# The second block's banded attention: scores as three float32r products of depth 64, two heads on the two row halves of the array

## The reference

```python
q, k, v = ...                      # of h @ w_in: (b,l,16*64), (b,l,4*64), (b,l,4*64)
s = einsum("bnqgrd,bnkgd->bgrnqk", qb, kb) * 64 ** -0.5      # 128 queries x 384 keys
valid = (abs(dist) <= 128) & (key >= 0) & (key < l)
s = where(valid, s - slopes * abs(dist), -inf)               # slope of head h: 2 ** (-8 (h+1) / 16)
m = maximum(max(s), sink)                                    # sink: one logit per head
p = exp(s - m)
probs = p / (sum(p) + exp(sink - m))
o = einsum("bgrnqk,bnkgd->bnqgrd", probs, vb)
```

## Time and profile before

| | us |
|---|---|
| median of 3 executions | 3427.03 |
| lowest, highest | 3340.12, 3492.56 |
| span of the profiled execution | 3498.2 |
| TensorE busy in it | 2989.8 (85%) |
| VectorE busy | 1504.5 (43%) |
| ScalarE busy | 972.0 (28%) |
| mean granted TensorE clock | 0.854 |

### The profile page before, as it was taken

The page is one execution under the profiler, slowest core; times in us unless marked ns, Lnnn a source line. Parts: engine busy times, 40 slices in busy tenths (PEclk is TensorE's granted clock), DMA queues, the critical chain, the costliest instruction groups (busy, mean ns, idle before and its releaser), DMA issues. The chain is left out here.

```text
span 3498.2 us, 37554 instructions
## 1 busy us (share of the span) xinstructions
PE 2989.8 (85%) x13760; PEld 2374.7 (68%) x13760; DVE 1504.5 (43%) x3662; ACT 972.0 (28%) x2200; POOL 196.1 (6%) x203
## 2 busy tenths in 40 slices
PE   3999957999565939899999998896696699999996
PEld 3888846779454728766666885772584588887875
DVE  3111367667888131244444114558413341424244
ACT  2121242446543121232222123450311321212121
POOL 1000020000200010000000000226000000000000
PEclk8999865999797969855555999699798799999998
DMA  2121200000001221000000120001213111111113
GB/s 83 49 73 50 86 1 1 1 1 2 1 1 48 97 74 50 19 7 13 7 13 34 49 73 28 1 1 54 82 49 118 43 48 49 49 49 46 50 47 117
DMA packets 91655, 144.86 MB, mean 41 GB/s; under 512 B 34256, under 2 KB 40528, under 8 KB 91472
## 3 DMA queue, kind: packets, MB, share of 16 engines
q1 hardware_dynamic: 84304, 117.28, 11.0%
q0 software_dynamic: 4864, 16.78, 1.2%
q10 hardware_dynamic: 2304, 8.39, 0.6%
HBM read 117.25 MB, written 25.17 MB: 41 GB/s over the span
## 5 line engine op out<-in xcount | busy, mean ns | idle before, releaser
L368 PE MATMUL banks<-h3T,mlwhi 128*128 128x512 f32 x1024 | 318.4, 392 | 9.4 <-DVE mlwlo L334 6.1
L368 PE MATMUL banks<-mlwhi,fT 128*128 128x512 f32 x1024 | 316.1, 390 | 3.3 <-ACT relu L2140 3.3
L368 PE MATMUL banks<-g1whi,hT 128*128 128x512 f32 (+1 forms) x1024 | 302.0, 378 | 5.7 <-DVE g1wlo L334 5.7
L334 DVE TENSOR_TENSOR mlwlo<-mlraw,mlwhi 128x512 fp32r<-128x512 f32 x128 | 87.7, 691 | 464.4 <-ACT mlwhi L311 464.4
L368 PEld LDWEIGHTS banks<-h3T,mlwhi 128*128 128x128 f32 x1024 | 192.9, 189 | 52.6 <-DVE mlwlo L334 6.5
L311 ACT ACTIVATE mlwhi<-mlraw 128x512 fp32r<-128x512 f32 x128 | 80.8, 632 | 526.9 <-PE banks L368 522.6
L368 PEld LDWEIGHTS banks<-mlwhi,fT 128*128 128x128 f32 x1024 | 191.6, 188 | 45.7 <-ACT relu L2140 6.3
L368 PEld LDWEIGHTS banks<-g1whi,hT 128*128 128x128 f32 x1024 | 189.2, 189 | 41.3 <-DVE g1wlo L334 6.1
L1053 PE MATMUL banks<-k2T,q2T 64*128 64x384 f32 (+1 forms) x256 | 194.1, 870 | 9.7 <-PEq L1495 9.7
L368 PE MATMUL banks<-h3T,mlwlo 128*128 128x512 f32 x512 | 200.1, 391 | 0.0
L368 PE MATMUL banks<-mlwlo,fT 128*128 128x512 f32 x512 | 199.2, 389 | 0.0
(11 more groups left out here) (448 smaller groups left out, 5760.2 us busy)
## 6 DMA issues: line engine op xcount, KB each, us to landing
mlraw<-in_w_up SPq DMA_DIRECT2D x64, 256.0 KB, 2.8
mlraw<-in_w_down SPq DMA_DIRECT2D x64, 256.0 KB, 2.7
g1raw<-in_w_in SPq DMA_DIRECT2D x56, 256.0 KB, 2.6
g3raw<-in_w_in SPq DMA_DIRECT2D x40, 256.0 KB, 2.6
g4raw<-in_w_out SPq DMA_DIRECT2D x32, 256.0 KB, 2.6
xt<-in_x SPq DMA_DIRECT2D x8, 512.0 KB, 6.6
z_scratch<-zst POOLq DMA_DIRECT2D x16, 256.0 KB, 2.6
cw<-in_cmp_w SPq DMA_DIRECT2D x2, 2048.0 KB, 9.2
```

The lines of the kernel that those rows point to most:

```text
L334: nc.vector.tensor_tensor(wlo[n % RING][:, w_slice(n)], raw[n % RAW][:, w_slice(n)], f32(whi[n % RING][:, w_slice(n)]), ALU.subtract).then ...
L368: last = nc.tensor.matmul(out, l, r, start=(k == 0 and i == 0), stop=(k == job.nk - 1 and i == 2))
```

## The change

In g2, q and k are kept as float32r pairs: `q2T` and `k2T` become two tensors each, high part written by ScalarE, low part by VectorE (product minus high part), for every accumulator. A query row half holds head j and the other half head j+8, so that the k job needs each key head once: 256 columns, four accumulators, where there were 512 and eight. q is scaled by 0.125 / slope of its head, with a table `qscale` that 16 small memsets write in a block of its own ahead of g2. The weights of the q jobs come in two transfers a step with 256-byte pieces.

The ALiBi table is one [128, 384] tile without slopes; the custom operation multiplies by the negated slope instead and takes a minimum.

The attention has its own function, `window2_stage`. Scores are issued for two heads together: three float32r products of depth 64 for each, alternating between the row halves, in two PSUM banks. Values are 64 columns wide. The sink's exp, the sum, the reciprocal and the scaling are done for four heads at once. VectorE's copy of the transposes of u-2 stands behind the bias operations of u+3 and u+4.

```diff
 def window2_tables(nc, sem, mem, C, kb, tmp_kb):
-            for h in range(ATT_HEADS):
-                nc.vector.tensor_scalar(tab[:, h, :], base[:], 2.0 ** (-8.0 * (h + 1) / ATT_HEADS), None,
-                                        ALU.mult).then_inc(dve_s, 1)
+            nc.vector.tensor_copy(tab[:], base[:]).then_inc(dve_s, 1)
+def window2_stage(nc, sem, mem, ident, q_hi, q_lo, k_hi, k_lo, v2, tab, nsink, x_kb, pt_kb, st_kb, yt, y_free, psum,
+                  store):
+    X, AHEAD, LAG = 6, 4, 2
...
+            def scores(u):
...
+                if u >= 4:
+                    pe.wait_ge(m_ready, u - 2)
+                for n, (q, k) in enumerate(((q_hi, k_hi), (q_hi, k_lo), (q_lo, k_hi))):
+                    for b in range(2):
+                        rows = slice(64 * b, 64 * b + 64)
+                        last = nc.tensor.matmul(psum[(u + b) % 4][:, 0:width(u)], q[rows, j, tok],
+                                                k[rows, j // 4, keys_at], start=(n == 0), stop=(n == 2))
+                        if n == 2:
+                            last.then_inc(s_ready, 1)
+            def transposes(u):
+                pe.wait_ge(e_ready, u + 1)
+                if u >= 2:
+                    pe.wait_ge(dev if u % 2 else aev, u // 2)
...
+            def values(u):
+                t, h = divmod(u, ATT_HEADS)
+                k0, k1 = keys(u)
+                pe.wait_ge(dev if u % 2 else aev, u // 2 + 1)
...
+            for u in range(NU):
+                if u % 2 == 1 and u + 3 < NU:
+                    scores(u + 3)
+                transposes(u)
+                if u >= LAG:
+                    values(u - LAG)
...
+            def output(w):
+                t, g = divmod(w, G)
+                cols = slice(4 * g, 4 * g + 4)
+                dve.wait_ge(k_ready, w + 1)
+                ch.link(nc.vector.tensor_tensor(tot[:, t, cols], tot[:, t, cols], sk[:, t, 1, cols], ALU.add))
+                ch.link(nc.vector.reciprocal(rec[:, t, cols], tot[:, t, cols]))
...
+            for u in range(NU):
+                if u + AHEAD < NU:
+                    bias_max(u + AHEAD)
+                if u >= 2 and u % 2 == 1:
+                    evacuate(u - 2)
+                if u >= 7 and u % 4 == 3:
+                    output(u // 4 - 1)
...
-               [cols_job(lambda j: qT[:, j, :], 0, C_Q, 0.125), cols_job(lambda j: qT[:, j, :], 4, C_Q + 512, 0.125),
-                cols_job(lambda j: kT[:, j, :], 0, None, 1.0, k_views),
+               [q_job(0), q_job(4),
+                Job(hT, KT, k_views, 256, False,
+                    act=Take(lambda e, ch, acc, ps, _: nc.scalar.activation(k_place(0, acc), ps[:, :], ACT.Copy)),
+                    dve=Take(k_lo), frees=lambda acc: "dve"),
```

More of the change, by code:

```diff
@@ L1484, in _, with window2_tables @@
             nc.vector.tensor_copy(C["trinegr"][:], C["trineg"][:]).then_inc(dve_s, 1)
-def window2_tables(nc, sem, mem, kb, tmp_kb):
+def window2_tables(nc, sem, mem, C, kb, tmp_kb):
     n = 3 * P
-    tab = mem.at("wtab", kb, [P, ATT_HEADS, n], F32)
+    tab = mem.at("wtab", kb, [P, n], F32)
+    nsink = mem.at("wnsink", kb + 1.5, [P, ATT_HEADS], F32)
     ramp = mem.at("wramp", tmp_kb, [P, n], I32)
@@ L1513, in _ @@
             ch.link(nc.vector.tensor_tensor(base[:], base[:], neg[:], ALU.min))
+            nc.vector.tensor_scalar(nsink[:].rearrange("p (j b) -> p j b", b=2),
+                                    C["sink"][:].rearrange("p (b j) -> p j b", b=2), -1.0, None,
+                                    ALU.mult).then_inc(dve_s, 1)
             dve.wait_ge(pool_s, 3)
-            for h in range(ATT_HEADS):
-                nc.vector.tensor_scalar(tab[:, h, :], base[:], 2.0 ** (-8.0 * (h + 1) / ATT_HEADS), None,
-                                        ALU.mult).then_inc(dve_s, 1)
@@ L1954, in second_block @@
     w = a["w_in_2"][0]
-    qT = mem.at("q2T", 0, [P, ATT_HEADS // 2, SEQ], F32)
-    kT = mem.at("k2T", 32, [P, ATT_KV, SEQ], F32)
-    v2 = mem.at("v2", 48, [P, NT, ATT_KV * HD], F32)
+    qT = [mem.at("q2T", 32 * i, [P, ATT_HEADS // 2, SEQ], F32R) for i in range(2)]
+    kT = [mem.at("k2T", 72 + 8 * i, [P, ATT_KV // 2, SEQ], F32R) for i in range(2)]
+    v2 = mem.at("v2", 64, [P, NT, ATT_KV * HD], F32)
     dt_raw = mem.at("dt_raw", 184, [P, NT, 2 * SSM_HEADS], F32)
-    def cols_job(dst, j0, col, scale, wv=None):
+    qscale = mem.at("qscale", 183, [P, ATT_HEADS // 2], F32)
@@ new lines, in second_block, with _, q_place, q_job @@
+    qsc = sem("qscale")
+    with nc.Block() as block:
+        @block.vector
+        def _(dve):
+            for j in range(ATT_HEADS // 2):
+                nc.vector.memset(qscale[0:64, j:j + 1], 0.125 / slope2(j)).then_inc(qsc, 1)
+                nc.vector.memset(qscale[64:128, j:j + 1], 0.125 / slope2(j + ATT_HEADS // 2)).then_inc(qsc, 1)
+    def q_place(i, acc, j0):
+        return qT[i][:, j0 + acc // 2, (acc % 2) * 512:(acc % 2 + 1) * 512]
+    def q_job(j0):
+        return Job(hT, KT, [(lambda k, c=c: w[k * P:(k + 1) * P, C_Q + 512 * c + HD * j0:C_Q + 512 * c + HD * (j0 + 4)]
+                             .rearrange("p (j d) -> p j d", d=HD),
+                             lambda raw, c=c: raw[:, :].rearrange("p (j c d) -> p j c d", c=2, d=HD)[:, :, c, :])
+                            for c in range(2)], 512, False,
+                   act=Take(lambda e, ch, acc, ps, _: nc.scalar.activation(
+                       q_place(0, acc, j0), ps[:, :], ACT.Copy, scale=qscale[:, j0 + acc // 2:j0 + acc // 2 + 1])),
+                   dve=Take(lambda e, ch, acc, ps, _: nc.vector.scalar_tensor_tensor(
+                       out=q_place(1, acc, j0), in0=ps[:, :], scalar=qscale[:, j0 + acc // 2:j0 + acc // 2 + 1],
+                       in1=f32(q_place(0, acc, j0)), op0=ALU.mult, op1=ALU.subtract)),
+                   frees=lambda acc: "dve")
@@ L1961, in place, with k_place, k_lo, cols_job @@
+    def k_place(i, acc):
+        return kT[i][:, acc // 2, (acc % 2) * 512:(acc % 2 + 1) * 512]
+    def k_lo(e, ch, acc, ps, _):
+        return nc.vector.tensor_tensor(k_place(1, acc), ps[:, :], f32(k_place(0, acc)), ALU.subtract)
+    def cols_job(dst, j0, col, scale):
         def place(acc):
             return dst(j0 + acc // 2)[:, (acc % 2) * 512:(acc % 2 + 1) * 512]
-        return Job(hT, KT, wv or [(w_view(w, col, 512), 0)], 512, False,
+        return Job(hT, KT, [(w_view(w, col, 512), 0)], 512, False,
@@ L1968, in cols_job @@
                    frees=lambda acc: "act" if even(acc) else "dve")
-    k_views = [(lambda k: w[k * P:(k + 1) * P, C_K:C_K + 256].rearrange("p (g d) -> p g d", g=ATT_KV),
-                lambda raw, c=c: raw[:, :].rearrange("p (g c d) -> p g c d", g=ATT_KV, c=2)[:, :, c, :])
+    k_views = [(lambda k, c=c: w[k * P:(k + 1) * P, C_K + 2 * HD * c:C_K + 2 * HD * (c + 1)]
+                .rearrange("p (g d) -> p g d", d=HD),
+                lambda raw, c=c: raw[:, 0:256].rearrange("p (g c d) -> p g c d", c=2, d=HD)[:, :, c, :])
                for c in range(2)]
@@ L1978, in second_block, with y_free @@
     gemm_stage(nc, sem, "g2", mem, 153,
-               [cols_job(lambda j: qT[:, j, :], 0, C_Q, 0.125), cols_job(lambda j: qT[:, j, :], 4, C_Q + 512, 0.125),
-                cols_job(lambda j: kT[:, j, :], 0, None, 1.0, k_views),
+               [q_job(0), q_job(4),
+                Job(hT, KT, k_views, 256, False,
+                    act=Take(lambda e, ch, acc, ps, _: nc.scalar.activation(k_place(0, acc), ps[:, :], ACT.Copy)),
+                    dve=Take(k_lo), frees=lambda acc: "dve"),
                 Job(hT, KT, [(w_view(w, C_V, 256), 0), (w_view(w, C_DT, 32), 256)], 288, True, act=Take(v_act),
                     frees=lambda t: "act")], psum)
-    tab = window2_tables(nc, sem, mem, 56, 153)
-    yt = [mem.at("yt", 171 + 4 * i, [P, DM], F32) for i in range(2)]
+    tab, nsink = window2_tables(nc, sem, mem, C, 171, 153)
+    yt = [mem.at("yt", 174 + 4 * i, [P, DM], F32) for i in range(2)]
     y_st = [sem(f"y_st{i}") for i in range(2)]
[L1987 to L2001, removed]
+    def y_free(dve, t, g):
+        if g == 0 and t >= 2:
+            dve.wait_ge(y_st[t % 2], 16 * (t // 2))
     def store(sp, o_done):
         for t in range(NT):
-            sp.wait_ge(o_done, ATT_HEADS * (t + 1))
+            sp.wait_ge(o_done, ATT_HEADS // 4 * (t + 1))
             sp.dma_start(scr_y[t * P:(t + 1) * P, :], yt[t % 2][:]).then_inc(y_st[t % 2], 16)
@@ L2008, in store @@
             sp.wait_ge(y_st[i], 16 * NT // 2)
-    attention_stage(nc, sem, "w2", mem, C, units, 1, [big[:, 0:1024], big[:, 1024:2048]], psum, 80, 153, 167,
-                    store=store, width=3 * P, slots=6, ahead=4, lag=2)
+    window2_stage(nc, sem, mem, C["ident"], qT[0], qT[1], kT[0], kT[1], v2, tab, nsink, 153, 162, 168, yt, y_free, psum,
+                  store)
     xraw = mem.at("xraw", 0, [P, XBC_TILES, SEQ + 4], F32)
```

105 lines of the change are left out of this document (104 added, 1 removed).

## The result

The changed kernel takes **3463.72 us** (median of 4 executions, 3460.53 to 3465.23). The kernel before, run beside it, has a median of 3459.8 with the times 3340.12, 3427.03, 3492.56 and 3498.71. By medians nothing has moved. The ratio of the two is **1.0357** (95% interval 1.0332 to 1.0382), slower. One thing is needed to read it: the comparison leaves out executions of a kernel that lie over 1.5% above its fastest one, so here it sets the changed kernel against the 3340.12 alone.

The account below looks back on a forecast made before the run. It took the attention to be bound by TensorE at half clock, with VectorE's work newly exposed in each pair. Profiled span 3498 - 24 ahead of the attention + 21 in it = 3495, less 6: 3489 us; range 3345 to 3545.

Parts of the forecast that it names:

- How the numbers follow: Closing step giving outcome chances against the median 3427: faster than 3358 0.16, within 2% 0.50, slower 0.34.
- The paragraph on the median: On the kernel before: lowest execution has the attention at high clock, 156 us less (3342); the middle one half way.
- 0.25 of its 0.58: Whole kernel: low clock with chain had chance 0.58, of which 0.25 lay above the 3496 line, counted as slower.
- the size of the attention: Whole attention stage at the low clock: 452 or 476 us, taken as 455, +21 on 434.
- Scores up to VectorE's start: Attention, scores of a pair with 384 keys: 1.5 us if row halves overlap, 2.0 if not; 1.5 taken.
- score loads of the two halves 0.21 apart: Expected sign in the attention's profile after: weight loads of the two row halves' scores follow each other at 0.21 us.
- VectorE's piece: Attention, per pair of 384 keys: two bias operations, a copy, a small subtraction every second time and handovers, 2.07 us.
- less 6 for a timed execution: Whole kernel: 6 us subtracted from 3495, as the profiled span lay 6 us above the highest timed execution.
- part 1: Ahead of the attention: k job -21.6, table operations -4.0, memsets and block boundary +1.5; sum -24 us.
- The chain: Attention, each pair: scores, VectorE, then the rest of TensorE run one behind another; TensorE has nothing to issue for 2.07 us.
- the clock paragraph: Attention: weighed evidence for low or high clock and held to low; high clock had chance 0.13, back and forth 0.12.
- the chain is hidden: Rival for the attention: VectorE's work is hidden after all, pair 5.4 us, stage 330, total 3364; chance 0.03.

Follow-up runs that it names:

- the first experiment: The kernel before, unchanged, run again in five rounds to see its spread: 3493.16 us median of 6 (3350.38 to 3504.46), beside 11 more executions.

## Why the prediction was right or wrong

The forecast was 3489 and "within 2%"; the time is 3463.7, inside its range of 3345 to 3545, and the kernel is slower, by a ratio of 1.0357. Two steps failed, and they are of different kinds.

**The step that failed first is "How the numbers follow", where the result was measured against the median 3427.** The paragraph on the median had found that the lowest execution is one with the high clock in the attention, and that the change would be "judged against a mixture". The seventeen executions of the first experiment show that there is hardly a mixture: two groups, near 3345 and near 3497, with few between. 3427 was a rare time, not a middle. Against the upper group the changed kernel is 1% faster, against the lower 3.6% slower, and the ratio takes the lower. With the forecast's own 3489 the ratio to 3340 would have been 1.045. Seen from there the whole span that the forecast gave itself, 3465 to 3525, is slower, and not 0.25 of its 0.58. From a forecast of the low clock and a kernel before that sometimes has the high one, "slower" had to be the likeliest outcome, and I had the 3340 and its cause before me.

**The second is the size of the attention: +21 predicted, -19 measured**, with the mechanism right. By its terms, for a pair of 384 keys:

- Scores up to VectorE's start: 1.5 predicted, 1.37 measured (1605.45 to 1606.82). That it came out so near is luck in part. I had put six loads 0.21 apart, "so 1.28 at least", with VectorE one product early. The six take 0.82 us from the first start to the last end, as the loads of the two halves start together, and both heads are done at the same time. The sign "score loads of the two halves 0.21 apart" did not come true.
- VectorE's piece: 2.07 predicted, 1.78 and 1.97 measured (1599.88 to 1601.66, 1606.82 to 1608.79). I had taken 0.66 for each bias operation, the step from it to the next operation in the earlier trace rows. Two of them in a row start 0.54 apart: the next one doesn't wait for the first one's read of the accumulator.
- Two transposes, two values and what lies around them: 3.91 predicted, 3.79 measured.

Together 7.48 against 7.03, 48 x 0.45 = 22 us. With 256 keys it was 5.79 against 5.03, 12 us more: I had used the 1.5 of 384 columns for the scores of 256, which take 1.04 (1832.84 to 1833.88). A rounding to 455 and the ends of the stage make the rest of the 40. Against the total of 3489 two other terms work the other way: the rest of the program was 7 us longer, and the "less 6 for a timed execution" had no ground, since the timed median lies 3 us above the changed kernel's profiled span.

**Right:** part 1 came to -25.1 (predicted -24). The chain is what bounds the pair: TensorE busy for 0.73 (predicted 0.7), idle once a pair until L1663 is done; moving the copy took the wait away and nothing else was changed in that run. The low clock held in all four executions, 0.852 to 0.855, and the spread shrank from 159 us to 5. Value loads at 64 columns are still 333 ns each and 0.214 apart ((1.40 - 0.33) / 5), as at 128. The Trainium skill ("TensorE: Matmul & The Clock Gate", section "LDWEIGHTS (loading the stationary operand)") gives the load as columns over 1.2 GHz, which is 107 ns for 128. The kernel with the early copy agrees with that at the high clock ((0.75 - 0.19) / 5 = 0.11, with six value loads in 0.75 us and 192 ns for one); at the low clock loads follow each other at twice that, 0.214. The halves overlap: 1.33 us for six products, against 1.92. The Trainium skill (the same page, "Part 3: Packing small matmuls") has products on different tiles of the array run at the same time, and the trace agrees.

**What I had right without its weight:** the clock paragraph named the idle piece of 2 us as speaking for the low clock. In the new stage with narrow values it decided. With it: low in every execution of three kernels, by mean clock, and by stretch in the three traces. Without it: high in every execution, from about 40 us into the stage. But it isn't the only thing. With the idle piece and wide values the clock went up and down. The old stage has no idle piece, is at 100 of 100 and stays low for 305 us in one trace and for all of it in the other, and so it does with narrow values. That last kernel and the one with the early copy are both narrow and without a gap, 0.50 and 1.00; what still differs between them is the scores, one fp32 product on one row half at a time against float32r products on two, and the small operations. No run has the scores alone, so their part in the clock is untested. TensorE's busy share by itself doesn't tell the clock in these rows; what it follows stays open here. The Trainium skill (the same page, "Part 1: The HAM clock gate") has activity release the throttle. The stage with the early copy agrees, since it rose in unbroken work; the old stage, 434 us at 0.50 with TensorE full, doesn't. The rival "the chain is hidden", 3364, priced only the idle time; with the clock it is 3234. (It was also counted among the outcomes faster than 3358, which 3364 is not.)

## What to carry to other kernels

When two products of a group are issued together, look at each in-order queue that consumes them: a small operation that releases the *previous* group must stand ahead of those that wait for the new one. One misplaced copy cost 120 us of idle time here and, through the clock, 110 more. Where a kernel's executions fall into two groups, plot time against the granted clock before anything is predicted, and say which group the change will be compared with. In a stage at the low clock, "fewer columns" isn't a saving by itself: it can bring next to nothing at that level (3.58 us a unit for 3.69 here) and, as the six executions with narrow values suggest without proving it, take away the chance of the other.

## What was not expected of the hardware

- The same program has executions of 3493 to 3504 us, with this stage at 1.2 GHz throughout in the one traced, and others of 3344 to 3350, whose higher mean clock (0.896 to 0.899 against 0.853 to 0.857) says that much of it ran at 2.4 GHz. In a third kind it changed over in mid-stage, after 305 us of unbroken work.
- Useless columns made a kernel faster: 84 us with the idle piece in place, and 6 us without it up to the next stage's start, both through the clock.
- The pace of weight loads follows the granted clock: 0.214 us at 0.50, 0.11 at 1.00.
- Two float32r products of depth 64 on different row halves run at once whichever is issued first: 1.33 us for six of 384 columns in either order, against 1.92 in a row. Their weight loads come in pairs as well, six in 0.82 us, where loads on full rows follow each other at 0.21.
- Two custom operations of VectorE with an accumulator start 0.54 us apart although one takes 0.62 by its row; a different operation behind one starts 0.66 later when it reads the accumulator, 0.54 when it doesn't (L1663 at 1600.96).
